# Layer 1's merge stage: one of the four sums of h is made on GpSimd, beside VectorE

## What is computed

```python
h = rms_norm(x, g_pre)
u = jnp.einsum('bsd,dn->bsn', h, w_in)
(..., merge) = jnp.split(u, _split_points(), axis=-1)
proj = jnp.einsum('bsnw,nwd->bsnd', branches, w_branch)
gates = jax.nn.sigmoid(merge.reshape(b, s, N_BRANCH, D_MODEL))
merged = jnp.sum(gates * proj, axis=2)
```

## Time and profile before

| | before |
|---|---|
| median of 3 runs | 2430.54 us (2430.44 to 2434.85) |
| the profiled execution | 2432.14 us |
| its span | 2430.3 us, of which 1.8 us lie around it |
| TensorE busy | 2311.3 us (95%) |
| VectorE busy | 1603.9 us (66%) |
| ScalarE busy | 1030.0 us (42%) |
| GpSimd busy | 434.2 us (18%) |
| mean granted TensorE clock | 0.985 of full speed |

### The profile page before, as it was taken

One profiled execution on the slowest core, in us unless ns is written; L12 is line 12 of the kernel. 1 busy time (PEld: TensorE's weight loads), 2 busy tenths in 40 slices (PEclk: granted clock), 3 DMA queues, 4 the chain that ended last, 5 costly groups with the idle time before them and its releaser, 6 DMA issues. The chain is left out here.

```text
span 2430.3 us, 32189 instructions
## 1 busy us (share of the span) xinstructions
PE 2311.3 (95%) x11512; PEld 1913.4 (79%) x11512; DVE 1603.9 (66%) x2011; ACT 1030.0 (42%) x1782; POOL 434.2 (18%) x401
## 2 busy tenths in 40 slices
PE   7999999989899999999999899997999999999997
PEld 6878878777678878887877788886887888888886
DVE  4557666566675545657687777874588777775556
ACT  4546455454433321233444455554333332334444
POOL 0233333334100000001232345540002000000000
PEclk9999999999999999999999899999999999999999
DMA  3101111110133264423332422202224444438764
GB/s 138 39 32 62 44 54 44 54 43 27 61 111 124 95 224 165 156 104 120 99 105 93 154 79 65 65 25 101 100 98 167 165 165 159 154 130 296 227 183 172
DMA packets 102620, 273.37 MB, mean 112 GB/s; under 512 B 9356, under 2 KB 35180, under 8 KB 98028
## 3 DMA queue, kind: packets, MB, share of 16 engines
q1 hardware_dynamic: 102508, 271.88, 32.5%
HBM read 196.03 MB, written 75.81 MB: 112 GB/s over the span
## 5 line engine op out<-in xcount | busy, mean ns | idle before, releaser
L79 PE MATMUL psG<-h_hi,w_hi 128*128 128x512 f32 x864 | 227.8, 402 | 5.9 <-ACT features_T L474 3.8
L79 PE MATMUL psG<-h_lo,w_hi 128*128 128x512 f32 x864 | 227.1, 402 | 0.0
L79 PE MATMUL psG<-h_hi,w_lo 128*128 128x512 f32 x864 | 223.1, 396 | 0.0
L79 PEld LDWEIGHTS psG<-h_hi,w_hi 128*128 128x128 f32 x864 | 159.2, 191 | 43.3 <-ACT features_T L474 4.8
L79 PEld LDWEIGHTS psG<-h_lo,w_hi 128*128 128x128 f32 x864 | 162.6, 193 | 33.0
L79 PEld LDWEIGHTS psG<-h_hi,w_lo 128*128 128x128 f32 x864 | 159.6, 189 | 32.2
L382 POOL TENSOR_TENSOR sb_e<-sb_e,sb_sp 128x128 f32<-128x128 f32 (+3 forms) x96 | 125.8, 1311 | 300.5 <-ACT sb_sp L417 300.4
L109 DVE TENSOR_TENSOR w_lo<-w_raw,w_hi 128x1024 fp32r<-128x1024 f32 x62 | 80.8, 1307 | 94.0 <-ACT w_hi L104 93.8
L556 DVE TENSOR_TENSOR sb_w_lo<-psT,sb_w_hi 128x512 fp32r<-128x512 f32 (+1 forms) x80 | 50.4, 630 | 110.7 <-ACT sb_w_hi L425 110.5
L104 ACT CAST w_hi<-w_raw 128x1024 fp32r<-128x1024 f32 x64 | 67.2, 1051 | 123.3 <-PE psG L79 73.0
L1949 POOL TENSOR_TENSOR features_T<-m_bias_both 128x512 f32<-128x512 f32 x10 | 16.0, 1596 | 539.1 <-DMA m_bias_both<-in_proj_pairs 491.8
(11 more groups left out here) (612 smaller groups left out, 5900.8 us busy)
## 6 DMA issues: line engine op xcount, KB each, us to landing
w_raw<-in_units SPq DMA_DIRECT2D x100, 512.0 KB, 3.7
w_raw<-hidden_blocks SPq DMA_DIRECT2D x77, 256.0 KB, 2.9
merge_gates<-features_T SPq DMA_DIRECT2D x12, 1024.0 KB, 7.3
merge_gates<-merge_gates SPq DMA_DIRECT2D x12, 1024.0 KB, 4.8
features<-features_T SPq DMA_DIRECT2D x24, 512.0 KB, 4.6
w_spare<-in_units SPq DMA_DIRECT2D x22, 512.0 KB, 4.2
hidden_blocks<-features_T SPq DMA_DIRECT2D x11, 1024.0 KB, 3.9
down_sums<-w_spare SPq DMA_DIRECT2D x22, 512.0 KB, 3.3
```

The lines of the kernel that those rows point to most:

```text
L79: return pe.matmul(out, lhs, rhs, start=first, stop=last, skip_group_check=True)
```

## The change

The three operations that make t3 leave VectorE's list and are put on GpSimd's, which waits for the end of the attention (`pv_done`, all of them) and for the last attention gate (`o_gated`), and signals by a semaphore of its own, `t3_done`. ScalarE's `turned(2)` waits for that semaphore. The counts of `turned_done` fall by three everywhere, and nothing else is changed.

```diff
+        t3_done = sem("t3_done")
+        hq = lambda t, r, c: t[:, 4 * r:4 * r + 4, c * HALF:(c + 1) * HALF].bitcast(F32)
+
+        @block.gpsimd
+        def _(pool):
+            t3 = t_raw[:, 2]
+            pool.wait_ge(L1.pv_done, len(BACKS))
+            pool.wait_ge(L1.o_gated, 4 * NC4)
+            pool.tensor_tensor(t3, hq(hT_hi, 1, 1), hq(hT_hi, 0, 1), ALU.subtract).then_inc(t3_done, 1)
+            pool.wait_ge(t3_done, 1)
+            pool.tensor_tensor(t3, t3, hq(hT_lo, 1, 1), ALU.add).then_inc(t3_done, 1)
+            pool.wait_ge(t3_done, 2)
+            pool.tensor_tensor(t3, t3, hq(hT_lo, 0, 1), ALU.subtract).then_inc(t3_done, 1)
...
             def turned(n, need):
-                act.wait_ge(turned_done, need)
+                act.wait_ge(t3_done if n == 2 else turned_done, need)
...
-                turned(2, 10)
+                turned(2, 3)
                 high(0, 0, 0)
                 plain_gate(2)
-                turned(3, 13)
+                turned(3, 10)
...
                 split_t(0)
                 W.split_lo(dve, U0 + 2)
-                turn(0, t3, hq(hT_hi, 1, 1), hq(hT_hi, 0, 1), ALU.subtract)
-                turn(8, t3, t3, hq(hT_lo, 1, 1), ALU.add)
-                turn(9, t3, t3, hq(hT_lo, 0, 1), ALU.subtract)
                 split_t(1)
                 W.split_lo(dve, U0 + 3)
                 split_t(2)
...
                     if m == 0 and q in (1, 2, 3, 5):
                         pe.wait_ge(t_hi_done, {1: 2, 2: 3, 3: 3, 5: 4}[q])
-                        pe.wait_ge(turned_done, {1: 11, 2: 12, 3: 12, 5: 14}[q])
+                        pe.wait_ge(turned_done, {1: 8, 2: 9, 3: 9, 5: 11}[q])
```

More of the change, by code:

```diff
@@ L974, in high @@
                     act.wait_ge(plain, 4)
-                    act.wait_ge(turned_done, 12)
+                    act.wait_ge(turned_done, 9)
+                    act.wait_ge(t3_done, 3)
                 act.copy(a_slot(q)[0], left(m % 2, q)).then_inc(a_hi_done, 1)
@@ L1110, in start @@
             def start():
-                hq = lambda t, r, c: t[:, 4 * r:4 * r + 4, c * HALF:(c + 1) * HALF].bitcast(F32)
-                t1, t2, t3, t4 = (t_raw[:, n] for n in range(4))
+                t1, t2, t4 = (t_raw[:, n] for n in (0, 1, 3))
                 def turn(need, dst, a, b, op):
@@ L1556, in layer2_projections @@
         a_hi_done, a_lo_done, s_done, made, p1_done, evac = B.a_hi_done, B.a_lo_done, B.s_done, B.prod, B.p1_done, B.evac
-        H0, TURNED0, TURN_HI0, RAW0 = MERGE_HALVES, 14, 4, 16 * MERGE_HALVES
+        H0, TURNED0, TURN_HI0, RAW0 = MERGE_HALVES, 11, 4, 16 * MERGE_HALVES
         MADE0, SUMS0, EVAC0 = 7 * H0, 4 * H0, 5 * H0
@@ L2751, in layer2_ffn @@
         plain, turned_done, t_hi_done, raw_here = B.plain, B.turned_done, B.t_hi_done, B.raw_here
-        H0, PLAIN0, TURNED0, TURN_HI0, RAW0 = MERGE_HALVES + len(PAIRS2), MERGE_PLAIN, 28, 8, 16 * (MERGE_HALVES + len(PAIRS2))
+        H0, PLAIN0, TURNED0, TURN_HI0, RAW0 = MERGE_HALVES + len(PAIRS2), MERGE_PLAIN, 25, 8, 16 * (MERGE_HALVES + len(PAIRS2))
         dw_here = [sem(f"dw_here{s}") for s in range(2)]
```

## The result

| | before | changed |
|---|---|---|
| median | 2430.6 us (5 runs, 2430.44 to 2434.85) | 2443.38 us (5 runs, 2442.76 to 2447.49) |
| span of the profiled execution | 2430.3 us | 2445.7 us |
| ratio | | 1.0054, 95% interval 1.004 to 1.0069 |

The interval of the ratio, 1.004 to 1.0069, is 9.7 to 16.8 us. The medians differ by 12.8 us. The forecast was 2441.0, in a range of 2436 to 2446.

The account below looks back on a forecast made before the run. TensorE, busy for 95% of the span, was taken as the bound. 13.05 us of new pause + 1.8 of clock - 4.37 gained = +10.5 us on 2430.54, giving 2441.0 us; range 2436 to 2446, bounds 2439.5 to 2445.

Parts of the forecast that it names:

- The pause and its worth: TensorE, before the first half's first product: 2.69 us idle plus 1.68 us at low clock, at most 4.37 us to gain.
- Taking turns: GpSimd and VectorE, both reading SBUF, alternate operations; each GpSimd operation of 2048 numbers delays VectorE by 4.35 us.
- Three turns ahead of the first `w_lo`: All three GpSimd operations get in before VectorE's first `w_lo`; it is 13.05 us late and TensorE stands still as long.
- The clock behind the pause: After TensorE's new 13.05 us pause in block 2 its clock stays low: 1.8 us lost, up to 3 allowed.
- What is gained behind it: At the first half, weights arrive ahead of TensorE, so its former pause and clock cost fall away: -4.37 us.
- The total: Whole kernel: 13.05 + 1.8 - 4.37 = +10.5 us, 2441.0 us against the median, 0.43% slower.
- The bounds: Whole kernel time between 2439.5 and 2445 us, given 0.76; the upper end has 5.2 us per GpSimd operation and 3 us of clock.
- No contention: Rival: VectorE runs undisturbed beside GpSimd, the full 4.37 us is gained, 2426.2 us, -0.18%; chance 0.12.
- GpSimd alone held up: Rival: VectorE always goes first, GpSimd ends t3 at 685.6; +5 us, or 6 with the clock, 2436; 0.10 shared with another rival.
- two turns instead of three: Rival: only two GpSimd operations get in before the first `w_lo`; +6.1 us, 2436.6; chance 0.10 shared with another rival.

Follow-up runs that it names:

- reordered kernel: Against the kernel before, nothing on GpSimd: VectorE makes t3 behind both `w_lo`, its `split_t` after sums and first rest; ScalarE's `high(0)` ahead of `turned(2)`; 2429.46 us, ratio 0.999.
- run with the late start: Changed kernel with one more wait: GpSimd begins t3 only when the first `w_lo` is done; 2442.45 us, ratio 1.0033.
- in pieces: Changed kernel with each of GpSimd's three operations cut into four of 512, ScalarE waiting for 12 signals; 2443.87 us, ratio 1.0037.
- run with memsets: Kernel before, VectorE keeping t3, plus three GpSimd memsets of 128 by 2048 into a place nobody reads; 2432.89 us, ratio 1.0001.
- run with one input: Kernel before, VectorE keeping t3, plus three GpSimd `tensor_scalar` operations reading one tensor, written where nobody reads; 2437.01 us, a single run.

## Why the prediction held

- **The pause and its worth.** Forecast: 2.69 us of pause and 1.68 of clock, 4.37 in all, and no more. The reordered kernel gained 4.42 us of the stretch. The sum holds, its second term is not all clock: at a granted clock of 1.00 the same 12 matmuls took 3.23 us behind a pause (last section), where without a pause they take 2.72 (687.46 - 684.74 in the reordered kernel). So of the 1.68 about 0.5 are lost at full clock too.
- **Taking turns.** Forecast from operations of 512 and 1024 numbers: 4.35 us for each of 2048. Measured 4.29, 4.24, 4.29, together 12.82 against 13.05. The line through the two sizes, 4.52 us, held at twice the larger one: 4.56 us in the run with the late start. What overlaps was taken as 0.2 us from the 512-number operations and is 0.3. By the 4497 ns of the Trainium skill (GPSIMD Engine Reference, Performance versus the Vector engine), less the same 0.2 us, the estimate was 4.3, as good. The Trainium skill's rule that the later one is blocked (SBUF — State Buffer, Who interferes with whom) held as well, with 6.58 against 2.29 us, and so did its exception for a GpSimd operation that only writes, with 2.29 us beside the memsets.
- **Three turns ahead of the first `w_lo`.** As laid out; it comes 12.84 us later (683.95 - 662.05 against 667.49 - 658.43), and TensorE resumes 12.78 us later.
- **The clock behind the pause.** Forecast 1.8, measured 1.63.
- **What is gained behind it.** The old pause and its clock are gone in full: 12.78 + 1.63 - 4.37 = 10.04, and the stretch has +9.95.
- **The total.** Forecast +10.5, in whole runs +12.8, with an interval from 9.7. The stretch explains 9.95 of it. The rest of some 3 us isn't explained by any wait that I found, so the forecast came within 2.4 us of the median without having that part: the parts ahead of the stretch and behind it differ by several us between any two profiles, in the kernels with the same code there too. The start of the stretch lies between 656.0 and 662.5 us in the nine profiles, and from its end to the end of the span there are 1739.8 to 1747.0 us. The rest has one sign throughout: in each of the seven kernels with several runs the change of the median is above the change of its stretch, by 1.6 us (reordered) to 5.3 us (in pieces), or to 4.2 us when measured to the third product. All of them are compared with one profile of the kernel before, whose clock fell; had it not fallen, its stretch would be some 1.1 us shorter, as in the run with memsets, and that much of the rest would go. Whether a part of what is left belongs to the change stays open.
- **The bounds.** The lower bound of 2439.5 does not follow from its terms: 3 x 3.96 + 1.8 - 4.37 = 9.3 gives 2439.9. Nothing hangs on the difference.
- **The rivals.** No contention, GpSimd alone held up, and two turns instead of three are all refuted by the timeline. A result that comes late plays no part in the changed kernel: ScalarE's rounding of t3 began at 681.91, ahead of both `w_lo`.

## What to carry to other kernels

Before work goes from VectorE to GpSimd, look at what VectorE does meanwhile. If its operations read two tensors from SBUF and GpSimd's read SBUF too, GpSimd's operation is put between two of them at nearly its full length (4.3 of 4.56 us), and a moved operation of 2.29 us comes back as one of 4.3 in front of whatever VectorE had next. Ask which result stands behind it in VectorE's list: here the added 12.8 us stood ahead of the first `w_lo`, for which TensorE waits, and the saved 6.9 behind it. When VectorE is late with one thing, first try to let it do that thing earlier; that gave all of the forecast gain in the stretch, with no engine added, though in whole runs it could not be told from nothing.

## What I had not expected

- **The clock's fall is not certain.** In the run with memsets TensorE paused for 2.64 us at the place where the kernel before pauses for 2.55, and its windows show the full clock throughout, where before it fell to 0.50:

```profile
684.00:686.00 2.00, 1.64 (x7) 1.00 0.41 172
686.00:688.00 2.00, 1.95 (x8) 1.00 0.00 0
```

  The 12 matmuls behind the pause took 687.60 - 684.37 = 3.23 us instead of 4.42. A pause of this size costs another 1.7 us in one execution and 0.5 us in another. What the 0.5 us at full clock are is not shown; the run with one input has the same 3.23 us (692.13 - 688.90) behind its pause of 1.18. This bounds what single profiles can tell of a few us, and may be one reason why the reordered kernel gains less in the median of runs than in its profile against that of before.
- **Smaller pieces shift the delay instead of removing it.** Cutting GpSimd's operations by four took two thirds from the first pause (3.9 instead of 12.6 us), since VectorE gives way once per operation of its own; but then GpSimd is the one that waits for VectorE between its first pieces (the first four take 13.22 us together, where one of this size takes 1.28 alone), and its result is 7.5 us later.
